# Streaming the 512 columns of a matrix product in another order, in the first down-projections of four feed-forward stages

## The reference

```python
def _swiglu_ffn(x, w_gate_up, w_down):
    g, u = jnp.split(x @ w_gate_up, 2, axis=-1)
    return (jax.nn.silu(g) * u) @ w_down
...
    for i in range(DEPTH):
        x = x + 0.5 * _swiglu_ffn(_rmsnorm(x, ffn1_norm[i]), ffn1_w_gate_up[i], ffn1_w_down[i])
...
        x = x + 0.5 * _swiglu_ffn(_rmsnorm(x, ffn2_norm[i]), ffn2_w_gate_up[i], ffn2_w_down[i])
```

## Time and profile before

| what | value |
|---|---|
| median of the runs | 3566.1 us |
| the runs | 3563.03 and 3569.16 us |
| span of the profiled execution | 3565.1 us |
| PE busy in it | 3457.4 us, 97% |
| matmuls in it | 20526 |
| mean granted TensorE clock | 0.985 of full |

### The profile page before, as it was taken

How to read it: one execution, slowest core, us unless ns; L and a number is a source line. 1 busy time by engine, 2 the same in 40 slices (tenths; PEclk the granted TensorE clock), 3 DMA queues, 4 the chain that set the end, 5 groups by cost and what they waited for, 6 DMA issues and landing times.

```text
span 3565.1 us, 55135 instructions
## 1 busy us (share of the span) xinstructions
PE 3457.4 (97%) x20526; PEld 3026.8 (85%) x20526; DVE 1676.3 (47%) x2652; ACT 1177.5 (33%) x2004; POOL 1339.1 (38%) x530
## 2 busy tenths in 40 slices
PE   7998999989989999999999989999999999999999
PEld 6998999989889999888877768888888877888887
DVE  5475534544755345542446654245433532734241
ACT  2465323324653223221235542222222234322122
POOL 3212343433123434344432224444444433344443
PEclk9999999999989999999999989999999999999999
DMA  3211232322113323232322113323332332223333
GB/s 106 72 43 54 84 97 84 98 62 71 37 54 88 94 83 96 76 102 86 101 82 60 54 53 89 100 88 100 89 100 88 98 89 79 83 89 94 94 94 94
DMA packets 570040, 294.88 MB, mean 83 GB/s; under 512 B 10663, under 2 KB 568358, under 8 KB 569782
## 3 DMA queue, kind: packets, MB, share of 16 engines
q1 hardware_dynamic: 568724, 291.36, 27.9%
q0 software_dynamic: 768, 1.11, 0.1%
q10 hardware_dynamic: 418, 0.62, 0.1%
HBM read 290.96 MB, written 2.10 MB: 82 GB/s over the span
## 4 chain that ended last, share of the span: by engine, by line
PE 61%; issue 27%; POOL 7%; DVE 3%; ACT 2%; POOLq 0%; DMA 0%; SPq 0%; ACTq 0%; DVEq 0%
PE big L2091 51%; POOL wlow L725 7%; PE big L2495 3%; PE big L2132 2%; PE misc L2145 1%; PE misc L2156 0%; DVE mix_lev L1595 0%; PE misc L2544 0%; PE misc L2182 0%; PE misc L2263 0%; ACT whigh L739 0%; DVE fresh L1571 0%; PE misc L2656 0%; PE big L2578 0%; PE misc L2196 0%
## 5 line engine op out<-in xcount | busy, mean ns | idle before, releaser
L725 POOL TENSOR_TENSOR wlow<-raw,whigh 128x1024 fp32r<-128x1024 f32 (+1 forms) x508 | 1328.9, 2616 | 2194.2 <-ACT whigh L739 2194.2
L739 ACT CAST whigh<-raw 128x1024 fp32r<-128x1024 f32 (+1 forms) x508 | 563.8, 1110 | 1986.8 <-PE big L2091 1803.5
L2091 PE MATMUL big<-ffn_x2l,whigh 128*128 128x264 f32 (+1 forms) x2016 | 540.2, 322 | 0.0
L2091 PE MATMUL big<-ffn_x2h,whigh 128*128 128x264 f32 (+1 forms) x2016 | 537.5, 321 | 2.1 <-DVE ffn_zg L1507 2.1
L2091 PE MATMUL big<-ffn_x2h,wlow 128*128 128x264 f32 (+1 forms) x2016 | 538.2, 321 | 0.0
L2091 PE MATMUL big<-xhigh,whigh 128*128 128x512 f32 (+1 forms) x1680 | 526.7, 351 | 0.8 <-POOL wlow L725 0.7
L2091 PE MATMUL big<-xlow,whigh 128*128 128x512 f32 (+1 forms) x1680 | 519.6, 347 | 0.0
L2091 PE MATMUL big<-xhigh,wlow 128*128 128x512 f32 (+1 forms) x1680 | 517.6, 346 | 0.0
L2091 PE MATMUL big<-ffn_hidl,whigh 128*128 128x264 f32 (+1 forms) x1408 | 421.4, 340 | 0.0
L2091 PE MATMUL big<-ffn_hidh,wlow 128*128 128x264 f32 (+1 forms) x1408 | 420.9, 339 | 0.0
L2091 PE MATMUL big<-ffn_hidh,whigh 128*128 128x264 f32 (+1 forms) x1408 | 419.1, 338 | 0.0
(11 more groups left out here) (405 smaller groups left out, 4131.0 us busy)
## 6 DMA issues: line engine op xcount, KB each, us to landing
raw<-in_ffn_w_gate_up SPq DMA_DIRECT2D x176, 512.0 KB, 3.7
raw<-in_ffn_w_down SPq DMA_DIRECT2D x96, 704.0 KB, 4.4
raw<-in_ffn_w_up SPq DMA_DIRECT2D x88, 512.0 KB, 3.7
raw<-in_w_in SPq DMA_DIRECT2D x52, 512.0 KB, 3.7
raw<-in_gmlp_w_in SPq DMA_DIRECT2D x32, 512.0 KB, 3.9
raw<-in_attn_w_in SPq DMA_DIRECT2D x24, 512.0 KB, 3.6
raw<-in_w_out SPq DMA_DIRECT2D x16, 512.0 KB, 3.7
raw<-in_gmlp_w_out SPq DMA_DIRECT2D x16, 512.0 KB, 3.7
```

Of the source, the lines that this page charges most:

```text
L725: eng.tensor_tensor(wlow[:, at0:at0 + n], raw[:, at0:at0 + n], whigh[:, at0:at0 + n].bitcast(F32), ALU.subtract).then_inc(slab_split, 1)
L739: eng.copy(whigh[:, at0:at0 + w], raw[:, at0:at0 + w]).then_inc(high_rounded, 1)
L2091: mm = eng.matmul(wide(big, slot, T)[:, c:c + n], w[:, (s * KC + k) * P:(s * KC + k + 1) * P], x[:, (x0 + k) * width + c:(x0 + k) * width ...
```

## The change

The products of the loop in the first half of the four later feed-forward phases take their 512 columns through a rearranged view, the same one for the operand that streams (`x`) and for the PSUM region that is written, so that each column still lands where it did. The table has one entry for each phase. "rows", n views the 512 columns as (512/n, n), in the order in which they lie. "between", n takes n columns of the left half of 256, then n of the right half, and so on: runs of n columns, and between two runs a jump of 256 columns (1 KB) forward or 256 - n back. Weights, waits, the number of matmuls and their sums are as before. The first pair of the four, the second half and all other products have `order=None`.

```diff
+ORDERS = [("rows", 256), ("between", 2), ("between", 16), ("rows", 16)]
...
+            def streamed(t, order):
+
+                if order is None:
+                    return t
+                how, n = order
+                if how == "rows":
+                    return t.rearrange("p (a b) -> p a b", b=n)
+                return t.rearrange("p (a b c) -> p b a c", a=2, c=n)
...
-                            mm = eng.matmul(wide(big, slot, T)[:, c:c + n],
+                            mm = eng.matmul(streamed(wide(big, slot, T)[:, c:c + n], order),
                                             w[:, (s * KC + k) * P:(s * KC + k + 1) * P],
-                                            x[:, (x0 + k) * width + c:(x0 + k) * width + c + n],
+                                            streamed(x[:, (x0 + k) * width + c:(x0 + k) * width + c + n], order),
...
-                    repeat(eng, 1, KD // 2, lambda i: plain_pair(down, tile0, i, T, hidh, hidl))
+                    order = ORDERS[ph[1]] if ph[0] == "ffn" and half == 0 else None
+                    repeat(eng, 1, KD // 2, lambda i: plain_pair(down, tile0, i, T, hidh, hidl, order=order))
```

More of the change, by code:

```diff
@@ L2082, in _, with slab @@
             ident = square("identity")
-            def slab(s, kc, xh, xl, T, slot, x0=0, width=T1, start=True, stop=True, before=None):
+            def streamed(t, order):
[5 more added lines that the diff above has]
+                return t.rearrange("p (a b c) -> p b a c", a=2, c=n)
+            def slab(s, kc, xh, xl, T, slot, x0=0, width=T1, start=True, stop=True, before=None, order=None):
                 for k in range(kc):
@@ L2104, in slot_free, with plain_pair @@
                     eng.wait_ge(tile_out[s], t2)
-            def plain_pair(st, tile0, i, T, xh=None, xl=None, before=None, width=T1):
+            def plain_pair(st, tile0, i, T, xh=None, xl=None, before=None, width=T1, order=None):
                 for s in range(2):
@@ L2109, in plain_pair @@
                     slot_free(s, tile0 // 2 + i)
-                    slab(s, st.kc, xh or xhigh, xl or xlow, T, s, width=width,
+                    slab(s, st.kc, xh or xhigh, xl or xlow, T, s, width=width, order=order,
                          before=before if s == 0 else None)
```

## The result

The changed kernel takes 3582.9 us (3582.44 and 3583.31) against 3566.1 before: a ratio of 1.0056, with a 95% interval of 1.0036 to 1.0076. That is 16.8 us more, where 45 were forecast and 3611 was the time. It is slower, clear of the noise and by under 2%, and it lies inside the stated range, but at little more than a third of the forecast effect.

A forecast was written before the change was run, and what follows sets the result against it. PE's matmul stream was taken to bound the kernel. Terms 45.4 (phase 1) + 0 + 0 + 0 took the span from 3565.1 to 3610.5 us, plus 1.0 for the median: 3611 (chance 0.45, 3606 to 3618); range 3562 to 3660.

The forecast's parts named there:

- What bounds the kernel: First down-projections of the four phases: time is PE's matmuls from start to start, and any change reaches the kernel's end.
- Phases 0 and 3 cost nothing: "rows" views in phases 0 and 3: the built instruction is the one of before, 0 us.
- Phase 1 at twice the column time: Phase 1's loop, runs of 2: 198 matmuls at 229 ns more each, +45.4 us, from ends of -3.8 and +45.4.
- Phase 2 at 0: Phase 2's loop, runs of 16: wastes nothing if accesses fetch more than two neighbouring values, so 0 us.
- The bound of 2.06 on the read from L2263: From strided matmuls at L2263: a strided column costs 1 to 2.06 times a contiguous one; writes assumed alike, with less trust.
- A stream already 7% short of the clock leaves nothing to absorb waste: Reason for phase 1's upper end, +45.4 us: float32r's feed or drain, not the array, was taken to be at its limit.
- No cost: Rival for phases 1 and 2: pairs are enough for both memories, views only change addresses; 3566 us, chance 0.33.
- Both in full: Rival: any broken PSUM write halves the column rate in all 396 matmuls, 90.8 us, 3657 us; chance 0.10.
- A price per jump: Rival: each step between runs costs one cycle, 21.1 us in phase 1, 2.6 in phase 2; 3590 us, chance 0.12.
- the sign that the prediction set for it: If phase 2's loop grows in the ratio 1 to 8 to phase 1's, the price is per jump.
- about 2%, 71 us: Whole kernel: the size of change that a measurement was said to tell from no change.
- The two sentences of the Trainium skill: One would slow both phases' matmuls for any non-contiguous pattern; the other, contiguous pairs suffice, would make both free.

The follow-up runs named there:

- e4_all_pairs: All eight down-projection loops read and write in pairs from the two halves, against the kernel before: 3715.0 against 3564.3 us, ratio 1.0428; each loop 64.87 us.
- e2: Eight views, one per loop, against plain 46.04 us: every second column 89.8, every fourth 91.3, pairs at a step of 4 89.8, single columns of two halves 42.7.
- e9: Read-side views of differing 16-byte line reuse, hidden tile fixed: pairs never returning to a line 95.5 us, pairs returning 64.7, runs of 4 from two regions 47.5.
- e8: Read side only, single columns j and j + D in turn, D from 4 to 1056 columns, one per loop, against plain: 42.73 us in all eight.
- e1: Read and write sides viewed separately, one view per loop: pairs read 64.87 us, pairs written 46.04, runs of 16 read 47.84, written 46.04; both sides in fours 50.09.
- e12: Write side alone in pairs in all eight loops, read plain, against the kernel before: every loop 46.04 us; 3566.7 against 3560.5 us, ratio 1.0014.
- e11: Eight new read-side views testing two readers against pairs needing different lines: 42.7 to 47.0 us, one 88.4; loop (1,0), j and j+3 at a step of 2, 47.0.
- e10: Single columns in turn for all 512-column products (four later feed-forward phases) and the first block's 264-column down-projections, against the kernel before: 3440.4 against 3562.7 us, ratio 0.9654.
- e6: All 512-column products of the four later feed-forward phases read single columns of two halves, DVE restores order, against before: 3464.8 against 3564.3 us, ratio 0.9720.
- e7: Hidden tile or weights fixed for all 11 pieces, and other views, against plain 46.04 us: tile fixed 46.2, weights fixed 46.04, both 46.2.
- e3: Narrower column widths per loop, plain or pairs, against 512: plain 384 34.7 us, plain 480 43.2, pairs of 256 33.2, of 384 48.9; runs of 8 over 512 48.2.

## Why the prediction was right and wrong

What bounds the kernel: right. PE's stream sets the time in these stretches, and e4_all_pairs makes eight times the loss of one loop into 1.0428 of the time. The loops of the change lose 20.6 us; the 16.8 between the medians is less by what the clock gave in this pair of measurements.

Phases 0 and 3 cost nothing: right, 46.04 us each.

Phase 1 at twice the column time, 45.4 us: wrong, and it is the term on which the time failed. It measured 18.8 us, and the loop 64.87 where about 91 were forecast. The step behind it, "a PSUM or SBUF access that fetches more than two neighbouring float32 values at a time would throw half of it away", names something real: pairs that leave half a line unused take 89.8 us a loop (e2), very near the 46.0 + 45.4 = 91.4 that the term gives. But the pairs of this change come back to the same line after one other pair, and that more than halves the price: 64.7 against 95.5 us for a loop in e9. I had looked at how much of a line a run uses, and not at when the rest of it is used.

Phase 2 at 0: nearly right, 1.8 us. That runs of 16 waste no line holds; the 22 cycles that a matmul with 32 runs takes over plain were not in the term, and their cause is open, since 8 runs of 64 cost nothing.

The bound of 2.06 on the read from L2263 held for steps of two and four columns and for sixteen and more regions: 85.5 to 91.3 us against 46.0 is 1.86 to 1.98. It did not hold for all: eight regions took 2.10, single columns of four regions with no line used twice 2.08 and pairs of two such regions 2.07. "The same bound with less trust" for PSUM writes was needless, the write is free.

"A stream already 7% short of the clock leaves nothing to absorb waste": the 7% is the read's, the feed of the two that I named ("feed or drain"), but it is no sign of a limit that every pattern hits. A reader that stays four turns in a line takes 518 cycles for 512 columns.

The rivals. That the time lay in the range says little, because the range was drawn around all of them. No cost: out. Both in full: out, the write isn't touched by the order and phase 2 lost 1.8 us. A price per jump came nearest in numbers, 3590 for 3582.9, with 21.1 and 2.6 us for the measured 18.8 and 1.8, and would have been the better forecast; but it isn't the mechanism, since a jump at every column runs faster than none (e2, e8). By the sign that the prediction set for it, phase 2 should have grown by an eighth of phase 1; it grew by a tenth. That is worth keeping in mind: two points, phases 1 and 2, nearly agreed with a rule that the nine loops of single columns from two places refuted. And "about 2%, 71 us" was too coarse for what a measurement tells: the interval of the result was 0.4% wide.

The two sentences of the Trainium skill, "Advanced Engine Details and Errata", section "Memory Cachelines": that any non-contiguous pattern of PSUM slows matmuls significantly doesn't hold for these writes, 46.04 us in pairs and in runs of 16 (e1, e12). That SBUF has lines of 16 bytes which need two hits each fits the large step in the table, if the hits are counted for even and odd columns apart and one after the other: by that count plain order has its two hits, 46.0 us, and two neighbouring columns by themselves have one, 89.8. It doesn't fit the ends: four such hits are faster still, 42.7, and one hit with the line soon seen again lies between, 53.7 to 64.9. The page doesn't say how to count. What it says of two consecutive elements it says of PSUM; that pairs are enough for the read as well was the prediction's reading, and the wrong one.

What was not settled. Whether there are two readers in the hardware is not shown; that the loops behave so is, and no run sets it against another mechanism than the rival of e11 and the theories before it. Why one turn and back after one other line costs 53.7 to 54.8 us with single columns and 64.7 to 64.9 with pairs, why runs of 16 cost 22 cycles more than plain ones and runs of 64 none, why runs of 4 took 47.5 in e9 and 50.1 in e1, and why (1,0) of e11 lies above its class are open.

## What to carry to other kernels

When PE is the bound and streams float32r, look at the distance between starts and not at the busy share: 0.2325 us for 512 columns looks full, and 7% of it is the order in which the operand is read. Read single columns of two places in turn, write PSUM plainly and let the engine that empties PSUM undo the order, if it isn't the bound; where a view must break up a row, break it at whole lines of 16 bytes, and never write off a pattern, or trust one, from the share of a line that it uses without asking when the rest is used. And put eight variants of a view into eight alike loops of one kernel: one profiled execution then compares them to a tenth of a microsecond, where whole-kernel times differ by several.

## What the runs showed of the hardware that was not expected

- A matmul of float32r over 512 columns takes 215.8 ns (518 cycles at 2.4 GHz) when it reads single columns from two places in turn, at each of nine distances from 4 to 1056 columns (e2, e8), and 232.5 ns in plain order. At 264 columns it is 112.5 (e10) against 121.4.
- Pairs from two places take 482 ns when their 16-byte lines are left for good, and 327 when they come back to them after one other pair (e9).
- Steps of two or four columns nearly double the time: 453 and 461 ns (e2).
- The order in which a matmul writes PSUM within a bank, in runs of 2 or 16, makes no difference: 232.5 ns each (e1, e12).
- VectorE reads 512 columns of PSUM at a step of two in 692 ns, the same as in a row (e6).
- Taking the same piece of the weights for all 11, in place of going on from piece to piece, leaves the 232.5 ns as they are (e7).
- In the loop of plain 128-column matmuls, which followed each other at 111 ns after its start, the granted clock fell to a mean of 0.59, and a matmul then took 213 ns (e3).
